# Two queues for the first loads, constants last, and another order of the six products of a row block

## What is computed

```
f1 = swiglu(rmsnorm(x, g0), w_gate, w_up, w_down)      # 1024 -> 2816 -> 1024
x  = x + 0.5 * rmsnorm(f1, g1)
x  = x + rmsnorm(mix(rmsnorm(x, g2)), g3)               # w_in, four head groups, w_out
f2 = swiglu(rmsnorm(x, g4), ...)
x  = x + 0.5 * rmsnorm(f2, g5)
```

## Time and profile before

| | us |
|---|---|
| median of 3 runs | 1209.89 (1205.71 to 1211.03) |
| profiled execution, own time | 1210.43 |
| its span | 1208.6 |
| TensorE busy | 1151.0 |
| VectorE busy | 626.6 |
| ScalarE busy | 336.8 |
| GpSimd busy | 40.2 |
| bytes moved | 92.23 MB, 76 GB/s over the span |

### The profile page before, as it was taken

One profiled execution on the slowest core, in us unless ns is written; L12 is line 12 of the kernel. 1 busy time (PEld: TensorE's weight loads), 2 busy tenths in 40 slices (PEclk: granted clock), 3 DMA queues, 4 the chain that ended last, 5 costly groups with the idle time before them and its releaser, 6 DMA issues.

```text
span 1208.6 us, 21735 instructions
## 1 busy us (share of the span) xinstructions
PE 1151.0 (95%) x8994; PEld 1128.4 (93%) x8994; DVE 626.6 (52%) x1075; ACT 336.8 (28%) x496; POOL 40.2 (3%) x57
## 2 busy tenths in 40 slices
PE   6999999999999997999898989999999999999996
PEld 6999999999999997998777889899999999999996
DVE  5533343333345775889767526865333343334346
ACT  5321222112223433521234343433122221122220
POOL 0000000000000000210221100000000000000001
PEclk9999999999999888999899989889999999999998
DMA  6313232223232211332500002203233232323222
GB/s 229 105 53 104 89 102 71 88 87 103 71 102 78 65 50 53 76 88 76 41 10 28 1 1 73 70 18 105 69 106 102 72 103 72 105 70 101 72 70 75
DMA packets 35391, 92.23 MB, mean 76 GB/s; under 512 B 10368, under 2 KB 12928, under 8 KB 35200
## 3 DMA queue, kind: packets, MB, share of 16 engines
q1 hardware_dynamic: 33744, 87.67, 24.5%
q10 hardware_dynamic: 1584, 3.68, 0.8%
HBM read 88.05 MB, written 3.28 MB: 76 GB/s over the span
## 4 chain that ended last, share of the span: by engine, by line
PE 83%; DVE 11%; issue 3%; ACT 2%; DMA 1%; ACTq 0%; DVEq 0%; SPq 0%
PE ps L305 24%; PE ps L307 24%; PE ps L306 24%; PE ps L1131 1%; DVE wl L289 1%; PE ps L1137 1%; PE ps L1138 1%; PE ps L367 1%; DVE mixf L984 1%; ACT wh L284 1%; DVE a L447 1%; PE ps L376 1%; DVE tb L676 1%; PE ps L1573 1%; DVE xx L1310 0%
## 5 line engine op out<-in xcount | busy, mean ns | idle before, releaser
L305 PE MATMUL ps<-xh,wh 128*128 128x272 f32 x1840 | 543.1, 295 | 24.9 <-DVE xl L503 11.0
L307 PE MATMUL ps<-xh,wl 128*128 128x272 f32 x1840 | 538.5, 293 | 0.0
L306 PE MATMUL ps<-xl,wh 128*128 128x272 f32 x1840 | 535.9, 291 | 0.0
L305 PEld LDWEIGHTS ps<-xh,wh 128*128 128x128 f32 x1840 | 352.9, 192 | 27.4 <-DVE wl L289 17.4
L306 PEld LDWEIGHTS ps<-xl,wh 128*128 128x128 f32 x1840 | 353.6, 192 | 0.1
L307 PEld LDWEIGHTS ps<-xh,wl 128*128 128x128 f32 x1840 | 352.4, 192 | 0.0
L284 ACT ACTIVATE wh<-raw 128x1024 fp32r<-128x1024 f32 (+1 forms) x163 | 167.8, 1033 | 322.1 <-PE ps L307 199.4
L289 DVE TENSOR_TENSOR wl<-raw,wh 128x1024 fp32r<-128x1024 f32 (+1 forms) x163 | 192.5, 1202 | 46.3 <-ACT wh L284 46.0
L305 PE MATMUL ps<-hh,wh 128*128 128x272 f32 x704 | 204.1, 290 | 0.0
L307 PE MATMUL ps<-hh,wl 128*128 128x272 f32 x704 | 203.6, 289 | 0.0
L306 PE MATMUL ps<-hl,wh 128*128 128x272 f32 x704 | 203.0, 288 | 0.0
(11 more groups left out here) (311 smaller groups left out, 855.4 us busy)
## 6 DMA issues: line engine op xcount, KB each, us to landing
raw<-in_w_gu SPq DMA_DIRECT2D x88, 512.0 KB, 3.7
raw<-in_w_d SPq DMA_DIRECT2D x32, 512.0 KB, 3.7
raw<-in_w_in SPq DMA_DIRECT2D x19, 512.0 KB, 3.7
raw<-in_w_d SPq DMA_DIRECT2D x16, 384.0 KB, 3.1
raw<-in_w_out SPq DMA_DIRECT2D x8, 512.0 KB, 3.7
x<-in_x ACTq DMA_DIRECT2D x8, 272.0 KB, 6.8
out_y<-x SPq DMA_DIRECT2D x16, 136.0 KB, 1.8
con<-in_con ACTq DMA_DIRECT2D x1, 1158.5 KB, 9.3
```

Of the source, the lines that this page charges most:

```text
L305: pe.matmul(out[:, n], wh[:, s, j], right_h[:, j, col], start=opens and j == order[0], stop=False)
L306: pe.matmul(out[:, n], wh[:, s, j], right_l[:, j, col], start=False, stop=False)
L307: last = pe.matmul(out[:, n], wl[:, s, j], right_h[:, j, col], start=False, stop=closes and j == order[-1])
```

## The change

In `product`, the loop over the kinds of product stands outside and the loop over the halves inside: wh with high for both halves, wh with low for both, wl with high for both. At the start, SP issues the first unit's load ahead of everything, then the parameters, the odd rows of x and the loads of units 1 to 3; its loop begins one iteration later. ACT issues the even rows of x only, and its three constant transfers stand behind its split of the second unit. The waits stay where they were.

```diff
--- before.py
+++ after.py
@@ -300,11 +300,11 @@
             for j in order:
                 if before:
                     before(j)
-                for n in parts:
-                    col = slice(n * H, n * H + H)
-                    pe.matmul(out[:, n], wh[:, s, j], right_h[:, j, col], start=opens and j == order[0], stop=False)
-                    pe.matmul(out[:, n], wh[:, s, j], right_l[:, j, col], start=False, stop=False)
-                    last = pe.matmul(out[:, n], wl[:, s, j], right_h[:, j, col], start=False, stop=closes and j == order[-1])
+                for left, right in ((wh, right_h), (wh, right_l), (wl, right_h)):
+                    first, final = left is wh and right is right_h, left is wl
+                    for n in parts:
+                        last = pe.matmul(out[:, n], left[:, s, j], right[:, j, n * H:n * H + H], start=first and opens and j == order[0],
+                                         stop=final and closes and j == order[-1])
             return last
 
 
@@ -712,10 +712,10 @@
                 pool.wait_ge(S("h_t"), row(5, 1, k) + 1 - KD)
                 pool.tensor_tensor(x[:, k, part_of(1)], x[:, k, part_of(1)], tb3[:, k % 3, part_of(1)], ADD).then_inc(S("y_pool"), 1)
 
-        def ffn_sp(sp, q, u0):
+        def ffn_sp(sp, q, u0, begun=0):
             u = u0
             for g, (f0, nf) in enumerate(GROUPS):
-                with sp.Fori(0, nf // 2) as i:
+                with sp.Fori(0 if g else begun, nf // 2) as i:
                     for s in range(4):
                         load(sp, u, i, s, a[f"w_gu{q}"][bass.ds(i * 4 + (2 * f0 + s), 1)].rearrange("a p n -> p (a n)"), KD)
                 u += 2 * nf
@@ -1971,8 +1971,13 @@
 
         @block.sync
         def _(sp):
+            load(sp, 0, 0, 0, a["w_gu0"][0], KD)
             sp.dma_start(par[:], a["par"]).then_inc(S("in_par"), 16)
-            ffn_sp(sp, 0, 0)
+            for k in range(1, KD, 2):
+                sp.dma_start(x[:, k], a["x"][:, k]).then_inc(S(f"in_x{k}"), 16)
+            for s in range(1, 4):
+                load(sp, 0, 0, s, a["w_gu0"][s], KD)
+            ffn_sp(sp, 0, 0, 1)
             mixer_sp(sp)
             ffn_sp(sp, 1, FFN2)
             for k in range(KD):
@@ -2003,15 +2008,15 @@
 
         @block.scalar
         def _(act):
-            for k in range(KD):
+            for k in range(0, KD, 2):
                 act.dma_start(x[:, k], a["x"][:, k]).then_inc(S(f"in_x{k}"), 16)
-            act.dma_start(con[:], a["con"]).then_inc(S("in_con"), 16)
-            act.dma_start(lora_w[:], a["lora"]).then_inc(S("in_con"), 16)
-            act.dma_start(dwbd[:], a["dw"]).then_inc(S("in_con"), 16)
             split_hi(act, 0, 0, 0, KD)
             act.wait_ge(S("in_par"), 16)
             first_act(act)
             split_hi(act, 0, 0, 1, KD)
+            act.dma_start(con[:], a["con"]).then_inc(S("in_con"), 16)
+            act.dma_start(lora_w[:], a["lora"]).then_inc(S("in_con"), 16)
+            act.dma_start(dwbd[:], a["dw"]).then_inc(S("in_con"), 16)
             act.wait_ge(S("in_con"), 48)
             ffn_act(act, 0, 0, 1)
             hand_over_act(act, 1, MIX0)
```

## The result

The changed kernel takes 1204.89 us (median of 17 runs, 1198.65 to 1208.98); the kernel before, run as often beside it, 1210.03 us (1202.81 to 1217.39). The ratio is 0.9949 with a 95% interval of 0.993 to 0.9968: faster by half a per cent, at the edge of what I had called "the same", and clear of no change by its interval.

The account below looks back on a forecast made before the run. TensorE, busy 95% of the span, was taken as the bound, through matmul distance and the first 11 us. Order 0 and start -0.7 us on 1210.4 gave 1209.7, said as 1209.3 in the runs' terms; range 1203 to 1223.

Parts of the forecast that it names:

- the same: Whole kernel: a time within about 0.5%, 6 us, of no change; chance 0.69.
- likeliest case: Whole kernel: order worth 0, start 0.7 us, so 1209.3 us, own range 1205 to 1214; chance 0.54.
- Part 1: New order of six matmuls per row block in the product: taken as 0 us.
- sign of being wrong: Stretch of whole products: 92 or more matmuls in 11 us, or 88 or fewer, would refute the order's forecast.
- rival D: Product: weights that stay are not paid again, 27 us gained for the added pairs, 1183 us; chance 0.11.
- rival B: Product: each bank change or weight repeat costs what duration rows hint, 13.6 us in sum, 1223 us; chance 0.17.
- The formula that was weighed: Single warm matmul in the product: N/2.4 + 2.5 ns, 115.8 ns here.
- Part 2: Start: first matmul from 11.02 to 8.4 us, but late constants leave 0.7 of 2.6 us gained.
- Rival C: Before the sums: the clock falls in TensorE's new 2 us wait, 2.5 to 3.4 us lost, 1214; chance 0.18.

Follow-up runs that it names:

- order_only: The kernel before with only the new order of the six matmuls, old start: 1205.91 us, ratio to before 0.9957.
- one_bank: The kernel before with all row blocks of half 0 ahead of those of half 1 in each product: 1210.09 us, ratio to before 1.0001.
- one_weight: The kernel before with the change's order, wl left out and wh with high computed twice: one run, no time given, 2401 matmuls between 100 and 400 us.
- narrow kernels: The kernels before and after, with 208 of 272 columns in every row block but a unit's first: one run each, no time given; 111.7 ns per matmul in the old order.
- start_only: The kernel after with the old order of the six matmuls, so the new start alone: 1214.13 us, ratio to before 1.0022.

## Why the prediction was right and where it was not

The time of 1204.89 us fell inside the range of 1203 to 1223, just under the likeliest case's own 1205 to 1214, and "within 0.5%" was the likeliest class; the ratio of 0.9949 stands on its very edge. The forecast of -0.7 us was too small by some 5 us, and one term of the sum is to blame. That the time still fell inside is luck as far as the order goes: its gain was forecast as nothing, and it happened to be about as small as what the prediction called "the same".

**Part 1 was mis-sized: 0 taken, 5.4 us by the count and 6.0 by the product of order_only.** The step that failed is "So neither a bank change nor a change of weights shows in the distance", from two windows with 90 matmuls each in 11 us. One matmul in 90 is 1.1%, or 1.4 ns of distance; the effect is 0.8 ns. The pair of rows could not have shown it. The sign of being wrong was as coarse: it asked for 92 matmuls or more in 11 us, and the effect gives 91, so it stayed silent. A second fault lies behind it: even a long one-bank stretch would have shown no difference from the old order, as one_bank does (2388 against 2387), because the gain is not proportional to the share of changes. The trace of before holds no stretch in which every matmul changes bank, so the bound had to stay open on both sides. It did, with -27 us as the lower end, but by another mechanism (weights not paid again, rival D), which one_weight refutes: 2401, and as many loads as ever.

**The upper bound, rival B, had the sign wrong.** It read the 2 ns by which L307 stands over L306 as the price of a bank change. No such price shows: the mean durations fell from 295, 293 and 291 ns to 293, 291 and 290 when the bank changed always. What the 2 ns come from is open.

**The formula that was weighed** (the Trainium skill, page "TensorE: Matmul & The Clock Gate", section "Back-to-back issue gap", an estimate of 115.8 ns here) is met by no run: 124.9 ns at best. The section gives it for a matmul by itself. What it says of streams, that load and matmul both set the spacing, goes with the narrow kernels, where 64 columns less gave 14 ns of the 27 that columns alone would give, though no run here shows the load's part in it.

**Part 2 was right in nearly every point.** Forecast and measured: wh of unit 0 at 5.2 and 5.49; first matmul 8.4 and 8.64; con issued when the second weights have landed, 11.3 and 11.82, and not when ACT's engine is done with them (12.59 + 1.04); last constant 17.8 and 17.64 (12.84 + 4.8); end of the adds 24.75 and 24.64; sums 24.75 and 24.78. The table load did hide. TensorE came to the sums at 23.5 and not at 22.8, so its wait is 1.3 us and not 2. Its first matmul was 0.24 us later than forecast, and its clock rose later: a pair of matmuls still takes 0.66 us at 13.77 and 0.42 at 14.55, so the rise lies 5.6 us behind the first matmul, where I had put 5. In start_only it came after 4.2 us (0.43 at 12.62, 0.29 at 13.06), and there the wait was 1.74 us. The gain at the sums is 0.65 us, forecast 0.7.

**Rival C was real.** It had a chance of 0.18, and start_only shows it in its trace and in its runs. It was not in the changed kernel's profiled execution; whether it is in some of its 17 runs, no trace of them is there to tell.

**The profiled execution overstates the change.** Of its 11.7 us, some 5.4 are the order and 0.65 the start. Most of the rest goes with the clock, 0.971 against 0.967 over the span, which is an estimate of 5 us. The largest piece is a stretch at half clock that the kernel before has in its second hand-over and the kernel after lacks: between the 5701st and the 5901st matmul the lead of the kernel after grows from 4.8 to 9.6 us. Before, then after:

```profile
787.00:798.00 11.00, 10.67 (x49) 10.67 (x50) 7.43 (x23) 2.67 (x7) 0.00 (x0) 0.53 0.14 50
```

```profile
782.00:798.00 16.00, 15.57 (x126) 15.57 (x127) 13.56 (x37) 5.69 (x13) 0.00 (x0) 1.00 0.11 34
```

## What to carry to other kernels

Before a pair of counts is called equal, work out what one more in the count would mean: effects of half a per cent need windows of many hundreds of matmuls, and there the count came back to within one in the traces of different kernels with the same order. When two accumulations run side by side in two PSUM banks, let them alternate matmul by matmul: it cost nothing here and gave 0.6% more matmuls in a dense stretch at 272 columns (next to nothing at 208), while putting equal weights next to each other added nothing to it. And what starts an engine earlier is worth only what the next wait leaves; here one wait for constants, placed ahead of work that does not read them, held back three quarters of it.

## What the runs showed of the hardware that I had not expected

- A gain of 0.8 ns per matmul (125.7 to 124.9 ns at 272 columns) from changing the PSUM bank, and with it the half of the columns, with every matmul (2402 matmuls in 300 us against 2387), and none from changing it after every third against once in 24 (2387 and 2388).
- A distance of 111.7 ns at 208 columns and 125.7 at 272: 14 ns for 64 columns, where 64 columns at 2.4 GHz would be 27.
- ACT's DMA instructions behind an ACTIVATE go out before that ACTIVATE runs: con was issued at 11.82 us, when the second weights had landed (issued at 4.32, 7.5 us to landing), while wh of that unit started at 12.59.
- The scatter of 0.9% between runs of one kernel goes with the granted clock: 1198.65 us at 0.971, 1208.98 at 0.965.
